# A two-layer decoder trunk on one core: the norm's roots moved behind the projections, x loaded as columns, the sums in two passes, the latents later

## The chip, the core and the metric

The kernel runs on one core of a Trainium2 chip. The core has TensorE (PE in the profile; its weight loads are listed as PEld), VectorE (DVE), ScalarE (ACT), GpSimd (POOL) and SyncE (SP), whose queue issues most of the loads. The engines run their own programs and wait for each other through semaphores. The metric is the device time of one execution in microseconds (us); lower is better.

## The reference

x is (1, 256, 1024) in fp32 and goes through two layers:

```python
h = rms_norm(x, attn_norm[i])
proj = h @ w_in[i]
# A: stick-breaking attention, B: latent attention (MLA), C: sliding window with sinks,
# D: block-sparse (MoBA); 4 heads of 64 each, all from slices of proj
...
x = x + groups.reshape(B, S, MIX_WIDTH) @ w_o[i]
h = rms_norm(x, ffn_norm[i])
u = causal_depthwise_conv(h @ w_up[i], conv_w[i], conv_b[i])
x = x + (jax.nn.silu(u[..., :D_FF]) * u[..., D_FF:]) @ w_down[i]
x = x + (p[i] @ ple_proj[i]) * jax.nn.sigmoid(x @ ple_gate[i])
```

`rms_norm(x, g)` is x times the reciprocal root of its row's mean square, times g. Group A takes z = q k^T / 8, and its weights are exp(log_sigmoid(z) + tail), where tail is the sum of log_sigmoid(-z) over the later keys before the query. Group B projects to a q latent (192) and a kv latent (128), normalises both and projects them up.

## The kernel before

The 256 tokens are two tiles t of 128 rows. The weights come in units of up to 128 x 2048 in fp32, loaded by SP into a ring of six buffers (`raw`), in the order of use. Most products are done in two parts of reduced-width fp32 (fp32r): ACT copies a unit to `wh` (`high(u)`, L539), the high part, and DVE (L1441) or, from the MLP on, POOL (L418) subtracts it from the unit to give `wl` (`low(u)`), which lies where `raw` was. A product is then three matmuls, high by high and the two mixed ones (`split_product`, L859 to L861). Only the units M_MLA_A, M_MLA_B and the one of ple_proj are multiplied whole in fp32, which PE does in two records per matmul. The activations are held as columns: `hT`, with high and low parts `hT_h` and `hT_l`.

There is no scheduler: each engine's order is the order of its program. The places that matter here, in each layer:

- **Start.** SP loads x, the gain row and the weights. ACT squares x (L520), POOL makes the root of each row (L425 to L428), DVE multiplies x by root and gain to `hn` (L1393), PE transposes `hn` (L908), ACT and DVE copy it to `hT`, and PE multiplies the MLA columns (L874) before the first split unit, M_SB_Q. In layer 1 the same chain begins at the end of layer 0, where DVE adds the last term to x (L1733).
- **After M_SB_Q.** PE transposes the convolution's taps (L998) and p (L1005), which were loaded as rows, and the two latents (L1012); then M_SB_K, the MLA up-projection (L1027 to L1029), M_SB_V, M_MOBA_Q, the stick-breaking scores (L1045 to L1054), M_MOBA_K and so on.
- **MLA.** From the up-projection ACT copies q and k/v and squares them, DVE sums the squares (L1599, L1602), POOL takes the power (L410), DVE scales the keys (L1615 to L1620). On DVE `low(6)` and `low(7)`, for M_MOBA_K and M_SWA_Q, stand behind that.
- **Stick-breaking.** ACT makes log(1 + exp(-|z|)) through three tables, DVE adds max(z, 0) (L1629), and PE subtracts the running sums by multiplying with a triangle of -1 (`neg_tri`, L1083, L1089) and with `neg_ones` (L1085), in fp32.

The projections' results leave PSUM through ACT copies (`copied`, L559). Unit numbers: 2 M_SB_Q, 3 M_SB_K, 4 M_SB_V, 5 M_MOBA_Q, 6 M_MOBA_K, 7 M_SWA_Q, 8 M_SWA_KV.

Of the kernel before, what the change touches and what calls it, by code (L numbers as in the profile page):

```python
# [15 lines left out]
P = 128  # L16
# [5 lines left out]
H = 4  # L22
# [22 lines left out]
G_ATTN, G_FFN, G_GROUP = 0, D, 2 * D  # L45
# [56 lines left out]
def _cols(n):  # L102
# [25 lines left out]
    "x_squared": 8, "roots": 12, "hn_ready": 8, "xT_ready": 12, "hT_act": 2, "hT_dve": 2,  # L128
    "xT_high": 12, "xT_low": 12, "pr_ready": 7, "squared": 7, "sums_ready": 4, "ssk_ready": 1,
    "lat_done": 2, "lat_T": 2, "cT_ready": 2, "mla_up": 2, "mla_up_ready": 4, "v_ready": 6,  # L130
    "mla_qk": 2, "mla_T": 2, "mT_ready": 4, "conv_T": 1, "conv_ready": 1, "moba_qk": 1,
# [4 lines left out]
    "sb_log": 3, "sb_soft": 3, "sb_minus": 3, "sb_probs": 3, "groups_T": 4, "mix_ready": 4, "mix_low": 4,  # L136
    "wo_done": 3, "x_mid": 4, "tap2": 4 * STEPS, "tap1": 4 * STEPS, "conv_done": 4 * STEPS,
    "silu": STEPS, "prod": STEPS, "g_high": STEPS, "g_low": STEPS, "p_T": 1, "pT_ready": 1,
    "proj_done": 3, "pp_ready": 4, "down_done": 3, "x_mlp": 4, "gate_ready": 3, "sigmoid": 4, "ple_term": 4,
    "x_done": 4, "tables": 1, "sg_landed": 16, "uq_landed": 16, "uq2_landed": 16,  # L140
    "ukv_landed": 16, "conv_landed": 16, "p_landed": 16, "ng_landed": 16, "gain_landed": 16,
# [28 lines left out]
def build(nc, x_in, p_in, positions, w_in, w_uq, w_ukv, norm_gains, small_gains, w_o, w_up,  # L170
          conv_rows, w_down, ple_proj, ple_gate, out):
    with ExitStack() as ctx:
# [20 lines left out]
        ng = sb("ng", [P, 3 * D])  # L193
# [3 lines left out]
        p_sb = sb("p_sb", [P, TT, PLE])  # L197
# [6 lines left out]
        neg_ones = sb("neg_ones", [P, P])  # L204
        inv_freq = sb("inv_freq", [P, HD // 2])
# [20 lines left out]
        pb = sb("pb", [P, 1536])  # L226
        pt = sb("pt", [P, 1536])
        st = sb("st", [P, ST_ALL])
        conv_raw = sb("conv_raw", [2 * FT, 4, P])
# [12 lines left out]
        sb_e, sb_sp = pb, pt  # L242

# [16 lines left out]
        pos_landed = sem("pos_landed")  # L260
        out_landed = sem("out_landed")
        consts_made = sem("consts_made")
        rope_step, rope_arg, rope_sin = sem("rope_step"), sem("rope_arg"), sem("rope_sin")
# [8 lines left out]
        def load_small(eng, layer):  # L272

            eng.dma_start(sg[:], small_gains[layer].partition_broadcast(P)
                          ).then_inc(F["sg_landed"], 16)
            eng.dma_start(uq[:, 0, :], w_uq[layer][0:P, :]).then_inc(F["uq_landed"], 16)
# [3 lines left out]
            eng.dma_start(conv_raw[:], conv_rows[layer]).then_inc(F["conv_landed"], 16)  # L280
# [36 lines left out]
        def _(sp):  # L317
            for t in range(TT):
                sp.dma_start(x[:, t, :], x_in[0, t * P:(t + 1) * P, :]).then_inc(x_landed[t], 16)
            sp.dma_start(ng[:, 0:D], norm_gains[0, 0:D].partition_broadcast(P)  # L320
                         ).then_inc(F["gain_landed"], 16)
            for layer in range(DEPTH):
# [31 lines left out]
                if layer + 1 < DEPTH:  # L354
                    load_small(sp, layer + 1)
# [19 lines left out]
        def _(pool):  # L375
# [36 lines left out]
            for layer in range(DEPTH):  # L412
# [39 lines left out]
                for t in range(TT):  # L452
                    x_root(0, t)
                if layer == 0:
                    pool.wait_ge(F["roots"], 2)
# [4 lines left out]
                    pool.wait_ge(consts_made, 16)  # L460

# [37 lines left out]
                pool.wait_ge(F["hn_ready"], base["hn_ready"] + 8)  # L499
# [13 lines left out]
        def _(act):  # L513
            act.dma_start(pos_i[:], positions.rearrange("a (t p) -> p (a t)", p=P),
                          allow_slow_non_contiguous=True).then_inc(pos_landed, 16)

# [5 lines left out]

            for i in range(4):
                act.wait_ge(x_landed[i // 2], 16)
# [1244 lines left out]
```

## Time and profile before

| | |
|---|---|
| median of 3 runs | 708.56 us (708.23 to 708.64) |
| the profiled execution's own time | 710.84 us |
| its span, first to last instruction | 709.1 us |
| PE busy | 691.7 us, 98% |
| ACT, POOL, DVE busy | 390.4, 388.7, 331.2 us |
| bytes moved | 116 MB, 164 GB/s |

PE's busy time counts each matmul from its start to its modelled end, and these overlap, so a busy PE doesn't mean that it issues at its peak. The timeline shows when each piece starts. "x12" is the number of records; an fp32 matmul has two. The bracket at the end of a row is the idle time of the engine before it and who ended it.

### The profile page before, as it was taken

The page shows a single profiled execution, that of the slowest core. Times are in us where ns is not written, and L with a number is a line of the kernel's source. Part 1 is how long each engine was busy: PE and PEld are TensorE (multiplying, and loading weights), DVE is VectorE, ACT ScalarE, POOL GpSimd, SP SyncE. Part 2 cuts the span into 40 slices and gives each one's busy share as a digit, 9 for nine tenths or more (in the row PEclk, how much of TensorE's full clock was granted, in tenths as well). Part 3 has the DMA queues.
Part 4 walks back from the last instruction along what each step waited for, and adds up shares of the span by engine and source line. Part 5 has one row for each costly group of instructions (what it writes and reads, how often), then busy time and mean ns, then how long its engine had stood idle before and what let it go on. Part 6 is the DMA issues. An engine that isn't in the chain of part 4 may idle for free.

```text
span 709.1 us, 11731 instructions
## 1 busy us (share of the span) xinstructions
PE 691.7 (98%) x4628; PEld 622.6 (88%) x4628; DVE 331.2 (47%) x548; ACT 390.4 (55%) x578; POOL 388.7 (55%) x213
## 2 busy tenths in 40 slices
PE   4999999999999999999999999999999999999997
PEld 3889998789999999998858999886999999999985
DVE  3746676545433333335165576666343333333333
ACT  4658675466544445555346596546655445545542
POOL 4431200157888888888720222011698888887781
PEclk9999999999999999999999999999999999999999
DMA  9962212465565555554366511326455555555511
GB/s 292 350 226 90 90 60 83 157 229 189 187 196 194 189 178 177 178 184 145 108 208 213 190 60 62 118 82 215 144 183 194 193 179 177 178 183 195 184 31 59
DMA packets 78884, 116.11 MB, mean 164 GB/s; under 512 B 2343, under 2 KB 66727, under 8 KB 78591
## 3 DMA queue, kind: packets, MB, share of 16 engines
q1 hardware_dynamic: 77598, 112.46, 48.0%
q10 hardware_dynamic: 1248, 3.15, 1.1%
q8 instruction: 25, 0.41, 0.2%
q14 instruction: 13, 0.10, 0.0%
HBM read 114.55 MB, written 1.05 MB: 163 GB/s over the span
## 4 chain that ended last, share of the span: by engine, by line
PE 90%; DVE 3%; POOL 3%; ACT 2%; DMA 1%; issue 1%; SPq 0%; DVEq 0%; ACTq 0%
PE ps L859 23%; PE ps L861 23%; PE ps L860 23%; PE ps L874 3%; PE ps L1210 2%; POOL wl L418 2%; PE ps L943 2%; PE ps L980 2%; PE ps L908 1%; PE ps L963 1%; DMA ng<-norm_gains 1%; PE ps L934 1%; PE ps L973 1%; DVE pb L1708 1%; ACT wh L539 1%; DVE wl L1441 1%
## 5 line engine op out<-in xcount | busy, mean ns | idle before, releaser
L418 POOL TENSOR_TENSOR wl<-raw,wh 128x2048 fp32r<-128x2048 f32 (+1 forms) x72 | 324.5, 4539 | 88.0 <-ACT wh L539 88.0
L539 ACT ACTIVATE wh<-raw 128x2048 fp32r<-128x2048 f32 (+1 forms) x102 | 187.6, 1846 | 113.9 <-PE ps L861 107.9
L859 PE MATMUL ps<-hT_h,wh 128*128 128x256 f32 x752 | 213.2, 284 | 0.1
L860 PE MATMUL ps<-hT_l,wh 128*128 128x256 f32 x752 | 212.8, 283 | 0.0
L861 PE MATMUL ps<-hT_h,wl 128*128 128x256 f32 x752 | 212.8, 283 | 0.0
L859 PEld LDWEIGHTS ps<-hT_h,wh 128*128 128x128 f32 x752 | 144.3, 192 | 2.0 <-issue 0.9
L860 PEld LDWEIGHTS ps<-hT_l,wh 128*128 128x128 f32 x752 | 144.3, 192 | 0.6
L861 PEld LDWEIGHTS ps<-hT_h,wl 128*128 128x128 f32 x752 | 144.3, 192 | 0.0
L405 POOL TENSOR_SCALAR st<-st 128x2 f32<-128x2 f32 (+3 forms) x26 | 9.0, 345 | 160.0 <-ACT lat L586 74.6
L859 PE MATMUL ps<-wh,hT_h 128*128 128x256 f32 (+1 forms) x284 | 93.1, 328 | 0.0
L1708 DVE SCALAR_TENSOR_TENSOR pb<-ps,conv,pb 128x255 f32<-128x255 f32 (+1 forms) x96 | 39.7, 475 | 109.6 <-ACT pb L794 109.3
L861 PE MATMUL ps<-wh,hT_l 128*128 128x256 f32 (+1 forms) x284 | 90.2, 318 | 0.0
L860 PE MATMUL ps<-wl,hT_h 128*128 128x256 f32 (+1 forms) x284 | 90.1, 317 | 0.0
L1708 DVE SCALAR_TENSOR_TENSOR pt<-ps,conv,pt 128x255 f32<-128x255 f32 (+1 forms) x80 | 33.1, 476 | 97.3 <-ACT pt L794 97.2
L859 PE MATMUL ps<-wh,gT_h 128*128 128x512 f32 x192 | 75.3, 392 | 0.0
L860 PE MATMUL ps<-wl,gT_h 128*128 128x512 f32 x192 | 74.9, 390 | 0.0
L861 PE MATMUL ps<-wh,gT_l 128*128 128x512 f32 x192 | 74.8, 389 | 0.0
L1441 DVE TENSOR_TENSOR wl<-raw,wh 128x2048 fp32r<-128x2048 f32 (+1 forms) x30 | 64.1, 2148 | 16.3 <-ACT wh L539 16.2
L860 PEld LDWEIGHTS ps<-wl,hT_h 128*128 128x128 f32 x284 | 54.1, 191 | 4.4 <-issue 1.0
L859 PEld LDWEIGHTS ps<-wh,hT_h 128*128 128x128 f32 x284 | 54.1, 190 | 4.4 <-issue 1.0
L861 PEld LDWEIGHTS ps<-wh,hT_l 128*128 128x128 f32 x284 | 54.0, 190 | 3.7
L861 PEld LDWEIGHTS ps<-wh,gT_l 128*128 128x128 f32 x192 | 36.0, 188 | 7.7
(235 smaller groups left out, 895.7 us busy)
## 6 DMA issues: line engine op xcount, KB each, us to landing
raw<-w_up SPq DMA_DIRECT2D x44, 1024.0 KB, 5.1
raw<-w_down SPq DMA_DIRECT2D x22, 1024.0 KB, 4.9
raw<-w_in SPq DMA_DIRECT2D x16, 1024.0 KB, 9.0
raw<-w_o SPq DMA_DIRECT2D x6, 1024.0 KB, 4.9
raw<-ple_gate SPq DMA_DIRECT2D x6, 1024.0 KB, 4.8
raw<-w_in SPq DMA_DIRECT2D x4, 704.0 KB, 6.2
ng<-norm_gains ACTq DMA_DIRECT2D x2, 1024.0 KB, 6.5
raw<-w_o SPq DMA_DIRECT2D x4, 512.0 KB, 3.5
```

Source lines behind the costliest of these rows:

```text
L405: return pool.tensor_scalar(stat(a, n), stat(a, n), 1.0 / width, EPS, ALU.mult, ALU.add)
L418: pool.tensor_tensor(wl[:, slot, 0:n], raw[:, slot, 0:n], wh[:, u % RING, 0:n].bitcast(F32), ALU.subtract).then_inc(ffn_l_made, 1)
L539: act.activation(wh[:, u % RING, 0:n], raw[:, slot, 0:n], ACT.Copy).then_inc(h_made, 1)
L859: pe.matmul(dst, a_h, b_h, start=start, stop=False, skip_group_check=True)
L860: pe.matmul(dst, a_h, b_l, start=False, stop=False, skip_group_check=True)
L861: return pe.matmul(dst, a_l, b_h, start=False, stop=stop, skip_group_check=True)
L874: mm = pe.matmul(o, hT[:, k, tok], raw[:, slot, c], start=k == 0, stop=k == KT - 1, skip_group_check=True)
L943: pe.matmul(o, q(h)[:, P:SEQ], k(h)[:, 0:SEQ], start=(i == 0), stop=False, skip_group_check=True)
L980: mm = pe.matmul(ps[:, bank, 256 + h * HD:256 + (h + 1) * HD], pt[:, c:c + P], v(h, k), start=(k == 0), stop=(k == TT - 1), skip_group_che ...
L1210: mm = pe.matmul(ps[:, PROJ_BANKS[n], :], pT[:, k, t * P:(t + 1) * P], raw[:, slot, c], start=k == 0, stop=k == 1)
L1441: tt(wl[:, slot, 0:n], raw[:, slot, 0:n], wh[:, u % RING, 0:n].bitcast(F32), ALU.subtract).then_inc(l_made, 1)
L1708: stt(o, ps[:, bank + half, j * 256:j * 256 + SEQ - d], conv[:, tap, f], o, ALU.mult, ALU.add).then_inc(F[name], 1)
```

## The change

- **Roots in the copies.** The attention norm is no longer applied to x. `hT` is x as columns times the gain, and the root of a row's mean square is applied to the projections' results: where these have tokens in rows, ACT scales them as it copies (`rooted`, with a scale per row); where they are transposed (M_SB_Q, M_SB_K), DVE multiplies them by a row of roots, which PE makes from a diagonal of -root and `neg_ones`.
- **x as columns.** In layer 0 x is loaded a second time, transposed on the host, straight into `hT`, and DVE multiplies it by the gain there; PE transposes nothing. In layer 1 PE transposes x itself as its quarters are added, and DVE multiplies the gain in as it copies.
- **Embedding and convolution rows as columns.** Both are loaded in their transposed form; PE's transposes of them are gone.
- **Two passes.** The softplus is split into a high part (ACT, `sp_h`) and a low part (DVE, `pt_r`), and each fp32 matmul of the sums becomes two of fp32r.
- **Order of loads.** First half of x as columns, M_MLA_A, second half, M_MLA_B, M_SB_Q, then x by rows, and the small tables each before its use.
- **Latents later.** The latents' transposes stand behind M_SB_K, and the MLA up-projection behind M_SB_V.

```diff
 # SP
-            for t in range(TT):
-                sp.dma_start(x[:, t, :], x_in[0, t * P:(t + 1) * P, :]).then_inc(x_landed[t], 16)
-            sp.dma_start(ng[:, 0:D], norm_gains[0, 0:D].partition_broadcast(P)
-                         ).then_inc(F["gain_landed"], 16)
...
+                    if layer == 0 and u in (M_MLA_A, M_MLA_B):
+                        sp.dma_start(hT[:, k:k + n, :], x_cols[:, k:k + n, :]
+                                     ).then_inc(xT_landed[u], 16)
                     load(rows(w_in, k, n)[:, :, c:c + w], u)
-                    if layer == 0 and u == M_MLA_B:
-                        load_small(sp, 0)
+                    if layer == 0 and u == M_SB_Q:
+                        for t in range(TT):
+                            sp.dma_start(x[:, t, :], x_in[0, t * P:(t + 1) * P, :]
+                                         ).then_inc(x_landed[t], 16)
...
 # ACT
+                def rooted(dst, src, t, name, n, done):
...
+                    act.activation(dst, src, ACT.Identity, scale=stat(ST_X + 6 + t)
+                                   ).then_inc(F[done], 1)
...
                 for t in range(TT):
-                    copied(v_sb[:, t, :], ps[:, t, 0:256], "unit", M_SB_V, "v_ready")
+                    rooted(v_sb[:, t, :], ps[:, t, 0:256], t, "unit", M_SB_V, "v_ready")
                 high(6)
                 high(7)
...
+                for b in range(3):
+                    act.wait_ge(F["sb_soft"], base["sb_soft"] + b + 1)
+                    act.activation(sp_h[b], sb_sp[:, b * 512:(b + 1) * 512], ACT.Copy
+                                   ).then_inc(F["sp_high"], 1)
+                mT_out(0)
                 high(8)
-                mT_out(0)
...
 # PE
-                x_T(hn, AT_START, ("hn_ready", 0), quarters=(0, 1))
...
+                if layer == 0:
+                    pe.sem_inc(F["xT_ready"], 4)
+                    project_tile(M_MLA_A, 0, (0, 1), 0, after=1, part=(0, 1))
...
+                else:
+                    x_T(x, AT_START, None, quarters=(0, 1))
+                    project_tile(M_MLA_A, 0, (0, 1), 0, after=1)
...
                 project_T(M_SB_Q, 2)
 
-                for a in range(4):
-                    mm = pe.transpose(ps[:, 7, a * 44:a * 44 + 44], conv_raw[:, a, :],
...
+                pe.wait_ge(F["diag_made"], base["diag_made"] + 1)
+                pe.matmul(ps[:, 7, 256:512], neg_ones[:], tmp[:, 768:1024], start=True,
+                          stop=True, skip_group_check=True).then_inc(F["row_root"], 1)
+                project_T(M_SB_K, 3)
...
-                project_T(M_SB_K, 3)
+                pe.wait_ge(F["pr_ready"], base["pr_ready"] + 2)
+                project(M_SB_V, (0, 1), 0)
...
-                pe.wait_ge(F["pr_ready"], base["pr_ready"] + 2)
-                project(M_SB_V, (0, 1), 0)
                 pe.wait_ge(F["sbT_ready"], base["sbT_ready"] + 3)
                 project(M_MOBA_Q, (2, 3), 0)
...
-                pe.wait_ge(F["sb_soft"], base["sb_soft"] + 3)
+                pe.wait_ge(F["sp_low"], base["sp_low"] + 3)
...
-                        pe.matmul(o, neg_tri[:], sb_sp[:, i * 256:(i + 1) * 256], start=False,
-                                  stop=False, skip_group_check=True)
...
+                        pe.matmul(o, neg_tri_r[:], sp_h[b][:, j * 256:(j + 1) * 256],
+                                  start=False, stop=False, skip_group_check=True)
+                        pe.matmul(o, neg_tri_r[:], pt_r[:, i * 256:(i + 1) * 256],
+                                  start=False, stop=False, skip_group_check=True)
...
 # DVE
+                dve.wait_ge(F["roots"], base["roots"] + 2)
+                for t in range(TT):
+                    last = ts(tmp[:, 768 + t * P:768 + (t + 1) * P], ident[:],
+                              stat(ST_X + 6 + t), -1.0, ALU.mult, ALU.mult)
+                last.then_inc(F["diag_made"], 1)
+                low(3)
...
+                for b in range(3):
+                    c = slice(b * 512, (b + 1) * 512)
+                    dve.wait_ge(F["sp_high"], base["sp_high"] + b + 1)
+                    tt(pt_r[:, c], sb_sp[:, c], sp_h[b].bitcast(F32), ALU.subtract
+                       ).then_inc(F["sp_low"], 1)
                 low(8)
```

How this stands on the engines. First PE in layer 0 from the end of M_SB_Q to M_MOBA_Q; "..." stands for the matmuls of a product. Before:

```order
L861 MATMUL ps<-hT_h,wl 128x256
L998 MATMUL ps<-ident,conv_raw 128x44 x4
L1005 MATMUL ps<-ident,p_sb 128x128 [waits p_landed]
...
L859 MATMUL ps<-hT_h,wh 128x256 [waits l_made]
...
L1027 MATMUL ps<-uq,lat 128x384 [waits cT_ready,ukv_landed,conv_ready,uq2_landed,pT_ready,uq_landed,consts_made]
L1028 MATMUL ps<-uq,lat 128x384
L1029 MATMUL ps<-ukv,lat 128x512
...
L859 MATMUL ps<-wh,hT_h 128x256 [waits l_made,pr_ready]
...
L859 MATMUL ps<-wh,hT_h 128x256 [waits l_made,sbT_ready]
```

and now (`tmp` holds the diagonal of roots; the product that waits for pr_ready is M_SB_V, the one that waits for sbT_ready M_MOBA_Q):

```order
L1027 MATMUL ps<-tmp,neg_ones 128x256 [waits diag_made]
L877 MATMUL ps<-hT_h,wh 128x256 [waits l_made]
...
L1034 MATMUL ps<-ident,pr 128x128 [waits lat_done]
...
L877 MATMUL ps<-wh,hT_h 128x256 [waits l_made,pr_ready]
...
L1049 MATMUL ps<-uq,lat 128x384 [waits ukv_landed,cT_ready,uq2_landed,rrow_ready,uq_landed,consts_made]
L1050 MATMUL ps<-uq,lat 128x384
L1051 MATMUL ps<-ukv,lat 128x512
...
L877 MATMUL ps<-wh,hT_h 128x256 [waits l_made,sbT_ready]
```

M_SB_V moved from behind the up-projection to ahead of it, so that one product less stands between the up-projection and M_MOBA_K, and the first ten transposes went.

On DVE the steps of the MLA keys and the two `low` behind them (units 6 and 7) stand as they did; before:

```order
L1602 TENSOR_REDUCE st<-tmp 128x8
L1607 TENSOR_TENSOR lat<-lat,sg 128x768 [waits sums_ready]
...
L1615 TENSOR_TENSOR hT<-pr,st 128x8x64 [waits roots]
L1618 TENSOR_TENSOR hT<-hT,sg 128x8x64 [waits dve_step]
L1620 TENSOR_TENSOR hT<-kpe,st 128x8x32
L1441 TENSOR_TENSOR wl<-raw,wh 128x2048 [waits h_made] x2
```

and now:

```order
L1666 TENSOR_REDUCE st<-tmp 128x8
L1671 TENSOR_TENSOR lat<-lat,sg 128x768 [waits sums_ready]
...
L1679 TENSOR_TENSOR hT<-pr,st 128x8x64 [waits roots]
L1682 TENSOR_TENSOR hT<-hT,sg 128x8x64 [waits dve_step]
L1684 TENSOR_TENSOR hT<-kpe,st 128x8x32
L1484 TENSOR_TENSOR wl<-raw,wh 128x2048 [waits h_made] x2
```

Nothing moved within this piece; what it hangs on, the up-projection, is what moved on PE.

## Rows read from the trace of the kernel before

**Rows 1.** The page's busy times and its chain that ended last, by engine.

```profile
PE 691.7 (98%) x4628; PEld 622.6 (88%) x4628; DVE 331.2 (47%) x548; ACT 390.4 (55%) x578; POOL 388.7 (55%) x213
...
PE 90%; DVE 3%; POOL 3%; ACT 2%; DMA 1%; issue 1%; SPq 0%; DVEq 0%; ACTq 0%
```

**Rows 2.** Timeline of PE, 0 to 24.2 us: start, us, what, [idle before].

```profile
9.55 1.94 PE L908 MATMUL ps<-ident,hn 128*128 128x128 f32 x8 [9.55 <-DVE hn L1393]
11.42 5.89 PE L874 MATMUL ps<-raw,hT 128*128 128x352 f32 x12
17.15 1.04 PE L908 MATMUL ps<-ident,hn 128*128 128x128 f32 x8
18.02 6.08 PE L874 MATMUL ps<-raw,hT 128*128 128x352 f32 x20
24.04 0.36 PE L859 MATMUL ps<-hT_h,wh 128*128 128x256 f32 x1
```

**Rows 3.** Timeline of PE's weight loads; one of seven that start 0.59 us apart.

```profile
13.90 0.34 PEld L874 LDWEIGHTS ps<-raw,hT 128*128 128x128 f32 x1 [0.25 <-issue]
```

**Rows 4.** The gain row's transfer in the chain; transfers to 20 us; unit 2's landing.

```profile
1.73 6.90 DMA ng<-norm_gains
...
DMA packets 4205, 5.97 MB, mean 299 GB/s; under 512 B 444, under 2 KB 3520, under 8 KB 4204
...
DMA to landing us min/median/max: 12.1/12.1/12.1
```

**Rows 5.** Timeline of ACT and DVE: wh and wl of unit 2.

```profile
19.66 1.90 ACT L539 ACTIVATE wh<-raw 128x2048 fp32r<-128x2048 f32 x1
...
21.60 2.29 DVE L1441 TENSOR_TENSOR wl<-raw,wh 128x2048 fp32r<-128x2048 f32 x1 [1.10 <-ACT wh L539]
```

**Rows 6.** Timeline of PE between M_SB_Q and M_SB_K, in layer 0 and layer 1.

```profile
29.95 0.44 PE L998 MATMUL ps<-ident,conv_raw 44*128 44x44 f32 x4
...
32.27 0.36 PE L859 MATMUL ps<-hT_h,wh 128*128 128x256 f32 x1
...
377.99 0.44 PE L998 MATMUL ps<-ident,conv_raw 44*128 44x44 f32 x4
...
379.74 0.36 PE L859 MATMUL ps<-hT_h,wh 128*128 128x256 f32 x1
```

**Rows 7.** Timeline of PE: the last up-projection matmul, and M_MOBA_K's first.

```profile
41.54 1.02 PE L1029 MATMUL ps<-ukv,lat 128*128 128x512 f32 x2
...
57.33 0.36 PE L859 MATMUL ps<-wh,hT_h 128*128 128x256 f32 x1
```

**Rows 8.** Timelines of POOL and DVE: the power, the keys, low(6) and low(7).

```profile
48.24 3.02 POOL L410 TENSOR_TENSOR st<-st,neg_half 128x16 f32<-128x16 f32 x1
...
51.59 0.69 DVE L1615 TENSOR_TENSOR hT<-pr,st 128x512 f32<-128x512 f32 x1 [2.63 <-POOL st L439]
...
53.26 4.49 DVE L1441 TENSOR_TENSOR wl<-raw,wh 128x2048 fp32r<-128x2048 f32 x2
```

**Rows 9.** Timeline of PE in the sums; from the chain, ten 64-column records.

```profile
70.67 0.60 PE L1083 MATMUL ps<-pt,neg_tri 128*128 128x256 f32 x2
...
73.29 1.02 PE L1089 MATMUL ps<-pt,neg_tri 128*128 128x512 f32 x2
...
80.07 1.06 PE ps L1100 x10
```

**Rows 10.** Between the layers: DVE, PE, and a stretch (third number from the end: PEclk).

```profile
355.86 0.70 DVE L1733 TENSOR_TENSOR x<-x,hn 128x512 f32<-128x512 f32 x1
...
358.44 1.32 PE L908 MATMUL ps<-ident,hn 128*128 128x128 f32 x8 [1.35 <-DVE hn L1393]
359.87 5.48 PE L874 MATMUL ps<-raw,hT 128*128 128x352 f32 x12
...
372.08 0.35 PE L859 MATMUL ps<-hT_h,wh 128*128 128x256 f32 x1
...
360.30:363.80 3.50, 3.50 (x8) 2.03 (x7) 1.53 (x4) 1.79 (x5) 0.94 (x3) 0.52 1.12 354
```

More of the change, by code:

```diff
@@ L226, in build @@
         pb = sb("pb", [P, 1536])
+        with nc.sbuf_tensor("pt_r", [P, 1536], F32R) as pt_r:
+            pass
         pt = sb("pt", [P, 1536])
         st = sb("st", [P, ST_ALL])
-        conv_raw = sb("conv_raw", [2 * FT, 4, P])
         neg_half = sb("neg_half", [P, 16])
@@ L626, in _ @@
                                    ).then_inc(F["squared"], 1)
-                high(3)
-                if layer == 0:
-                    act.wait_ge(consts_made, 16)
-                for rows, heads in EVEN_ODD:
-                    copied(qk_sb[rows, heads, :],
-                           ps[rows, 2, :].rearrange("p (k n) -> p k n", k=2),
-                           "unit", M_SB_Q, "sbT_ready", scale=HD ** -0.5)
-                copied(pT[:], ps[:, 6, :].rearrange("p (k n) -> p k n", k=2), "p_T", 1, "pT_ready")
                 high(4)
@@ L690, in _ @@
                 for t in range(TT):
-                    copied(pr[:, 1, t, :], ps[:, 2 + t, :], "unit", M_MOBA_K, "pr_ready")
+                    rooted(pr[:, 1, t, :], ps[:, 2 + t, :], t, "unit", M_MOBA_K, "pr_ready")
                 act.wait_ge(F["pr_ready"], base["pr_ready"] + 4)
@@ L904, in x_T @@
                             pe.wait_ge(F[free], base[free] + 2 * t + 2)
-                        pe.wait_ge(F[ready[0]], base[ready[0]] + ready[1] + k + 1)
+                        if ready:
+                            pe.wait_ge(F[ready[0]], base[ready[0]] + ready[1] + k + 1)
+                        else:
+                            pe.wait_ge(F["x_done"], 4 * (layer - 1) + k + 1)
                         for j in range(4):
@@ L1589, in _, with sb_rooted @@
                     last.then_inc(F["lat_done"], 1)
-                dve.wait_ge(F["conv_T"], base["conv_T"] + 1)
-                dve.tensor_copy(conv[:], ps[:, 7, 0:176].rearrange("p (a n) -> p a n", a=4)
-                                ).then_inc(F["conv_ready"], 1)
-                low(4)
+                dve.wait_ge(F["row_root"], base["row_root"] + 1)
+                dve.tensor_copy(rrow[:], ps[:, 7, 256:512]).then_inc(F["rrow_ready"], 1)
+                def sb_rooted(rows, heads, bank, scale):
+                    c = ps[rows, bank, :].rearrange("p (k n) -> p k n", k=2)
+                    stt(qk_sb[rows, heads, :], c, scale,
+                        rrow[rows].unsqueeze(1).broadcast_to([rows.stop - rows.start, 2, SEQ]),
+                        ALU.mult, ALU.mult).then_inc(F["sbT_ready"], 1)
+                if layer == 0:
+                    dve.wait_ge(consts_made, 16)
+                dve.wait_ge(F["rrow_ready"], base["rrow_ready"] + 1)
+                unit_done(dve, layer, M_SB_Q)
+                for rows, heads in EVEN_ODD:
+                    sb_rooted(rows, heads, 2, HD ** -0.5)
+                unit_done(dve, layer, M_SB_K)
+                sb_rooted(slice(0, P), slice(H, H + 2), 3, 1.0)
                 low(5)
```

255 lines of the change are left out of this document (145 added, 110 removed).

## Prediction

> **What bounds the kernel now.** I read the page first: PE is busy 98% of a span of 709.1 us and carries 90% of the chain that ended last [rows 1]. PE's busy time is no measure of slack by itself, since pipelined matmuls overlap, so I went on to PE's timeline and asked of every stretch that the diff touches: when does PE start it, what does it issue there, and which engine's result comes last. Outside these stretches (output projection, MLP, gate) neither the work nor its order changes, so their time is taken as it is.
>
> PE's losses are few. The first transposes start at 9.55 us, the first product (the MLA columns) at 11.42, the first split product (unit M_SB_Q) at 24.04 [rows 2]. Between the layers PE waits 1.35 us for hn [rows 10]. The rest is work, so an edit pays only where it lets PE start earlier or issue less, and it costs where PE comes to a product whose wl part is not there.
>
> **Start of layer 0.** Before, x (1 MB) and the gain row (0.5 MB) land before the first weights. Now the first half of x as columns (0.5 MB) and the first weight unit (0.7 MB) are the first in the queue. The gain row, with 1.6 MB up to and with it, landed at 8.6 us [rows 4], so 1.25 MB should be there at about 7.5 us, and PE can start its first product then instead of at 11.42. Loads are issued in order and the queue holds the rest back: the third unit, issued at 7.06 us, took 12.1 us to land, at 19.2, with 5.1 MB issued up to and with it, against 5.97 MB moved in the first 20 us [rows 4]. In the new order 3.5 MB stand up to and with it, 1.6 MB less at 0.3 MB per us: it lands at about 14.4. ACT then makes wh in 1.90 us and DVE wl in 2.29 [rows 5]: ready at 18.7.
>
> PE's own path: 32 records of the MLA product. While PE had just started, a record took 0.59 us (the weight loads stand 0.59 us apart), later 0.30 (20 records in 5.98 us) [rows 2, 3]. The granted clock is printed as full there, but the spacing is that of the half level, 1.2 GHz, until about 15.7 us. From 7.5 us with a slow stretch of some 5 us and full speed behind it, PE needs 5 + (32 - 8.5) x 0.30 = 12 us, so it is at M_SB_Q at about 19.5, behind the 18.7 of DVE. **Start: 24.04 to 19.5, -4.5 us** (bounds: -3.0 if the slow records go on to 15.7 us as before and the third unit lands 1.5 us later; -5.3 if DVE's 18.7 is the end). The squares of x, the roots and the diagonal come behind the third unit's wh on ACT, about 5 us after it, and PE needs the diagonal only a product (5.8 us, 24.04 to 29.9 [rows 2, 6]) later: hidden, with about a microsecond to spare.
>
> **Between M_SB_Q and the next products.** In layer 0, 2.4 us pass from the end of M_SB_Q (29.9) to M_SB_K (32.27), with eight transposes of conv and p, six of the latents and waits for them [rows 6]. Six transposes stay (eight take 17.15 to 18.02 [rows 2], so 0.11 us each, 0.65). The new fp32 matmul of 256 columns for the row of roots has the shape of those of L1083, 0.44 us a piece; four of them with their 128-column partners take 2.62 [rows 9]. So 2.4 - 0.65 - 0.45 = **-1.3 us in layer 0**, and in layer 1, where the same stretch is 1.85 us (377.9 to 379.74), **-0.75 us**.
>
> **The MLA up-projection one product later.** This speaks against the change. From the last up-projection matmul (41.54) a chain runs over all engines: ACT copies and squares, DVE sums, POOL takes the power (48.24, 3.02 us), DVE scales the keys (51.59) and only then subtracts for units 6 and 7, since low(6) stands behind the keys on DVE: 4.49 us for two, so unit 6 is there at 53.26 + 2.29 = 55.5 [rows 7, 8]. That is 14.0 us after 41.54. PE comes to unit 6 (M_MOBA_K) at 57.33, 15.8 us after 41.54, with M_SB_V, M_MOBA_Q and the stick-breaking scores between: 1.8 us of slack. The new order puts M_SB_V ahead of the up-projection, so PE has only 15.8 - 5.8 = 10.0 us of work in that gap, while nothing in the chain gets shorter: ACT's squares don't wait for v_sb in either version, and v_sb and the wh of unit 6, which do get earlier, aren't last. PE should stand still for **4.0 us at M_MOBA_K, in each layer**. What is queued behind it on PE, the key product, its transposes and everything else, moves with it. Bounds: 0 if a step of the chain isn't needed where I read it, 4.5 if what is new on ACT and DVE ahead of the chain's first step delays it.
>
> What does such a wait do to PE's clock? Ahead of 359.87 us PE had 1.35 us idle, transposes and a short wait. From 360.3 to 363.8 the granted clock is 0.52, the lower of its two levels, 1.2 GHz, and twelve records took 5.5 us instead of 12 x 0.30 = 3.6 [rows 10]: 1.9 us lost, of which 0.1 to 0.2 is the modelled tail, so 1.8. A wait of 4 us is longer than that one, so I expect a half-speed stretch after each. Part of it may fall into the wait itself, so I take 1.2 us each, between 0 and 1.8: **+2.4 us in two**. The Trainium skill (TensorE: Matmul & The Clock Gate, Part 1) says that idleness takes the array to half clock and activity releases it; by its rule the lower bound of 0 falls away, and the trace agrees at the one place where it can be seen.
>
> **Stick-breaking sums.** Before, from 70.67 to the end of L1089's matmul at 74.15: four pairs in 2.62 us and one of 512 columns, 0.86 [rows 9]. Now each fp32 matmul becomes two of fp32r. The split products are of that type: 48 of 256 columns in 5.8 us, 0.12 each [rows 2, 6], so 0.24 at 512. At 128 columns no row of that type exists. The shortest fp32 matmuls in the trace, with 64 columns, follow each other at 0.11 us a record (ten in 1.06 us [rows 9]), as the 128-column ones do (0.22 for the two records of one), so the weight load seems to set it: I take 0.11. Bounds 0.06 (half the 256-column time) and 0.22 (no gain over fp32). Sum 4 x (0.24 + 0.22) + 0.48 = 2.3 us: **-1.2 us a layer**, between -0.3 and -1.6.
>
> The added copies on ACT (three, 0.6 us each) and subtractions on DVE (three, 0.7) stand ahead of wh and wl of unit 8, and PE waits for both. They cost nothing because the wait at M_MOBA_K comes first: in it ACT and DVE get ahead with the softplus. By my sum the last low part and wl of unit 8 are then ready some 0.3 us before PE comes to each. If that wait isn't there, this cover is gone too, and about 0.5 us a layer comes back.
>
> **Between the layers.** Before: the gate ends at 356.9 (358.44 less the idle time and the pipeline's tail), transposes of hn at 358.44 after the root, first product at 359.87, M_SB_Q at 372.08 [rows 10]. Now x is transposed as soon as it is added. The third addition on DVE ends at 356.56 [rows 10], so transposes run from 356.95, DVE scales the first quarter until 358.2 and PE starts the product there. 32 records at 0.30 and the eight transposes that are left, 0.9, are 10.5 us: M_SB_Q at about 368.7, if the clock holds, with wl of unit 2 ready some 0.3 us earlier. **-3.4 us** with the clock held, -1.6 without; PE idles only 0.4 us there, so I take the first.
>
> **Sum.** -4.5 - 1.3 + 4.0 - 1.2 = -3.0 in layer 0, -3.4 - 0.75 + 4.0 - 1.2 = -1.35 in layer 1, and 2.4 for the clock: -1.95 us. Against the profiled execution, whose span is 709.1 and whose own time is 710.84, that is a span of 707.15. The median of the three runs is 708.56, 2.3 under the profiled execution's time; taken from it, the forecast is **706.6 us**. About 0.2%, or 1.4 us (707.1 to 710.0), is what a measurement can tell from no change.
>
> **The rivals.**
> - *The waits come, the clock holds* (or drops once, cheaply): -1.95 - 2.4 = -4.35, so 704.2. For it: matmuls are dense ahead of the wait. Against: rows 10.
> - *No wait at M_MOBA_K*: the chain isn't bound to the up-projection as I read it. -4.35 - 8.0 = -12.35, with 1 us given back at the sums: 697.2. Against it: 14.0 against 10.0 us is a wide gap.
> - *The early gain is smaller*: the third unit lands 1.5 us later, or the clock still drops between the layers (+1.8): about 708.3, no change. The Trainium skill (TensorE: Matmul & The Clock Gate, Part 4) says that transposes don't count as activity for the gate; the trace shows a drop after a stretch mostly of them, and with its rule the drop would stay, and the time be that of this rival.
> - *Slower*: the two waits cost more than themselves. If PE comes out of each wait at half clock and needs two such stretches to get back, each costs 3.6 instead of 1.2, together +4.8: 711.4. It decides from 2.9 us a wait, where the sum passes +1.4. For it: the start shows some 4 us of slow records in a row. Against: between the layers one stretch was enough.
>
> **How the numbers follow.** Forecast 706.6 (705.2 to 708.2) 42%; clock holds 22%; smaller early gain 20%; no wait 8%; slower 8%. Range 701.5 to 709.6: it leaves out the slower rival and the case without a wait, and takes in all bounds of the start and the sums. Faster by over 0.2%: 0.61 (0.28 of the forecast's 0.42, the 0.22, the 0.08, 0.03 of the third); within: 0.31; slower: 0.08.
>
> **What would show it.** PE's first product at about 7.5 us and M_SB_Q at 19.5; an idle time of PE of about 4 us before M_MOBA_K in both layers, released by DVE's wl; a granted clock near 0.5 behind each and none between the layers; the sums in 2.3 us; M_SB_Q of layer 1 some 11.8 us after the gate's end instead of 15.2. If PE shows no wait at M_MOBA_K, the largest term is wrong; if M_SB_Q starts after 21 us, the loads are.

## The result, and the profile after

| | before | changed |
|---|---|---|
| median, us | 708.56 | 710.84 |
| profiled execution: span, us | 709.1 | 711.1 |
| profiled execution: mean granted clock | 0.997 | 0.990 |

The ratio is 1.0035, with a 95% interval of 1.0027 to 1.0044: the change costs 0.35%. The forecast was 706.6 us, with a range up to 709.6. The time lies outside it, on the side of the rival that had 8%. Of 17 executions of the changed kernel one took 1744 us, at a mean clock of 1.00; no trace of it exists, and it stands in none of the counts below.

The page's busy times and clock digits of the changed kernel stand beside [rows 1]:

```profile
PE 687.7 (97%) x4600; PEld 622.2 (87%) x4600; DVE 336.6 (47%) x560; ACT 390.1 (55%) x576; POOL 390.0 (55%) x213
...
PEclk9998999999999999999999899999999999999999
```

PE is busy for 4 us less and the span is 2 us longer. In the clock row (40 slices of 17.8 us, tenths of full speed) the digit 8 stands at two places, 53 to 71 and 391 to 409 us (the second stretch runs on into the next slice, see below). The waits of PE (what waited, for whom, us in total, times, longest) say where the rest went:

```profile
PE ps L891 <- DVE hT L1586: 9.5, 1, 9.5
PE ps L877 <- DVE wl L1484: 7.7, 2, 3.8
PE ps L1274 <- ACT hT_h L568: 0.9, 2, 0.5
PE ps L891 <- DVE hT L1419: 0.4, 1, 0.4
```

The second line is new: two waits of 3.85 us at M_MOBA_K, as the forecast had them. The first is the start: PE's first product begins at 9.49 us and not at 7.5. Now the timelines, which answer to [rows 2, 4, 5]. Of the start (DVE, ACT, then PE):

```profile
8.66 1.29 DVE L1586 TENSOR_TENSOR hT<-hT,gcol 128x512 f32<-128x512 f32 x2 [8.66 <-DMA gcol<-attn_cols]
...
16.65 1.89 ACT L552 ACTIVATE wh<-raw 128x2048 fp32r<-128x2048 f32 x1
...
18.58 2.29 DVE L1484 TENSOR_TENSOR wl<-raw,wh 128x2048 fp32r<-128x2048 f32 x1 [2.20 <-ACT wh L552]
...
9.49 12.39 PE L891 MATMUL ps<-raw,hT 128*128 128x352 f32 x32 [9.49 <-DVE hT L1586]
21.46 0.55 PE L877 MATMUL ps<-hT_h,wh 128*128 128x256 f32 x1
```

gcol, the gain as columns (8 KB), landed at 8.66 us. The first weights, issued at 1.26 and 7.3 us on their way, landed at about 8.6, also after the forecast's 7.5; DVE's multiplication by gcol then held PE until 9.49. From there PE took the 12.0 us of the forecast to M_SB_Q. The bytes moved in 40 slices of half a microsecond, 0 to 20 us:

```profile
GB/s 0 0 0 66 205 205 221 205 131 17 15 195 367 380 424 423 410 398 381 394 400 386 381 391 373 354 371 395 395 393 426 377 375 363 352 348 346 361 370 377
```

From 4.5 to 5.5 us almost nothing moves, though weights and the second half of x's columns still wait to be loaded.

PE around M_MOBA_K of layer 0, and the clock there (columns of the last two lines: stretch, its length, PE's busy time and matmuls, granted clock, DMA share, GB/s), against [rows 7, 10]:

```profile
43.50 1.02 PE L1051 MATMUL ps<-ukv,lat 128*128 128x512 f32 x2
...
57.56 0.58 PE L877 MATMUL ps<-wh,hT_h 128*128 128x256 f32 x1 [3.85 <-DVE wl L1484]
...
65.67 0.60 PE L1083 MATMUL ps<-ident,lat 128*96 128x128 f32 x4
...
55.90:62.70 6.80, 5.14 (x24) 0.50 0.00 0
...
404.04:410.80 6.76, 4.87 (x23) 0.50 0.00 1
```

From the last up-projection matmul to M_MOBA_K 14.06 us pass (forecast: 14.0). The clock is at its lower level, 1.2 GHz, for 6.8 us at each wait, twice as long as between the layers before. The first stretch begins at 55.9 us, 1.7 us before PE starts M_MOBA_K, so 5.1 us of it fall on work. M_MOBA_K takes 8.1 us instead of 5.8.

DVE in the same stretch shows the chain of [rows 8], unchanged, 2.0 us later: the keys after POOL's power, and low(6) behind them.

```profile
53.55 0.69 DVE L1679 TENSOR_TENSOR hT<-pr,st 128x512 f32<-128x512 f32 x1 [2.63 <-POOL st L456]
...
55.22 4.49 DVE L1484 TENSOR_TENSOR wl<-raw,wh 128x2048 fp32r<-128x2048 f32 x2
```

The sums, against [rows 9]: from 73.08 to the next product at 75.48, 2.4 us (forecast 2.3), no wait in them.

```profile
73.08 0.36 PE L1104 MATMUL ps<-gT_h,neg_tri_r 128*128 128x256 f32 x1
73.28 0.29 PE L1106 MATMUL ps<-pt_r,neg_tri_r 128*128 128x256 f32 x1
73.40 0.22 PE L1108 MATMUL ps<-gT_l,neg_ones_r 128*128 128x128 f32 x1
73.46 0.28 PE L1110 MATMUL ps<-pt_r,neg_ones_r 128*128 128x128 f32 x1
73.58 0.33 PE L1104 MATMUL ps<-gT_h,neg_tri_r 128*128 128x256 f32 x1
```

Between the layers, against [rows 10]:

```profile
358.20 1.03 PE L928 MATMUL ps<-ident,x 128*128 128x128 f32 x8
359.68 2.60 PE L891 MATMUL ps<-raw,hT 128*128 128x352 f32 x8 [0.44 <-DVE hT L1419]
...
370.01 0.37 PE L877 MATMUL ps<-hT_h,wh 128*128 128x256 f32 x1
...
361.00:364.00 3.00, 3.00 (x16) 1.00 1.10 358
```

M_SB_Q starts 11.8 us after the gate's end, as forecast, and the clock holds.

**Where the difference arises.** Start times of PE, changed less before, in the two profiled executions: M_SB_Q -2.6 (forecast -4.5); M_MOBA_K of layer 0 +0.2, behind the sums +1.3, M_SB_Q of layer 1 -2.1, M_MOBA_K of layer 1 +1.1, end +2.0.

**The clock of single executions.** The mean granted clock differs from execution to execution, and a stretch of 3.5 us at half level is 0.0025 of it (3.5 / 2 / 709). Of 19 executions of the kernel before, 14 have 0.999 or 1.000 and spans of 706.3 to 707.1, one 0.998 (707.5), four 0.997 (708.5 to 708.8). So the drop between the layers of [rows 10] is in few of them, and the profiled execution was one. Changed kernel: seven have 0.995 (two stretches, spans around 708.2), three 0.993 (708.8), six 0.990 (four stretches, around 710.8). The profiled execution is of the last kind. This turns out to be a part of the miss. Only the profiled executions show where their clock is low; the counts of stretches of the others are worked out from the mean, which also takes in the end of the span: in the kernel with matmuls in the wait, below, the profiled execution has 0.998, and only its last 2.3 us are low, when PE has nothing left to do.

### The profile page after: what moved, and what is told of

It reads as the page before. It is cut to its first block, busy times and chain, and to the rows that moved or that the text cites. A ratio compares the mean times of both kernels' runs of the same rounds, so it can differ in the third digit from the quotient of the medians.

```text
span 711.1 us, 11689 instructions
## 1 busy us (share of the span) xinstructions
PE 687.7 (97%) x4600; PEld 622.2 (87%) x4600; DVE 336.6 (47%) x560; ACT 390.1 (55%) x576; POOL 390.0 (55%) x213
## 4 chain that ended last, share of the span: by engine, by line
PE 92%; DVE 2%; POOL 2%; ACT 1%; DMA 1%; issue 1%; ACTq 0%; DVEq 0%
PE ps L877 24%; PE ps L878 24%; PE ps L879 24%; PE ps L891 3%; PE ps L1237 2%; PE ps L963 2%; PE ps L1000 2%; PE ps L983 1%; DMA gcol<-attn_cols 1%; PE ps L954 1%; POOL st L427 1%; PE ps L993 1%; PE ps L928 1%; POOL wl L435 1%; DVE wl L1484 1%
## 5 line engine op out<-in xcount | busy, mean ns | idle before, releaser
L877 PE MATMUL ps<-wh,hT_h 128*128 128x256 f32 (+1 forms) x284 | 94.7, 333 | 7.7 <-DVE wl L1484 7.7
L878 PE MATMUL ps<-wl,hT_h 128*128 128x256 f32 (+1 forms) x284 | 92.1, 324 | 0.0
L879 PE MATMUL ps<-wh,hT_l 128*128 128x256 f32 (+1 forms) x284 | 92.0, 324 | 0.0
L877 PEld LDWEIGHTS ps<-wh,hT_h 128*128 128x128 f32 x284 | 56.2, 198 | 12.1 <-DVE wl L1484 8.2
L878 PEld LDWEIGHTS ps<-wl,hT_h 128*128 128x128 f32 x284 | 56.3, 198 | 4.0 <-issue 0.5
L879 PEld LDWEIGHTS ps<-wh,hT_l 128*128 128x128 f32 x284 | 56.1, 198 | 3.6
L879 PEld LDWEIGHTS ps<-wh,gT_l 128*128 128x128 f32 x192 | 36.1, 188 | 7.7
```

The costliest lines, as they stand in the source:

```text
L877: pe.matmul(dst, a_h, b_h, start=start, stop=False, skip_group_check=True)
L878: pe.matmul(dst, a_h, b_l, start=False, stop=False, skip_group_check=True)
L879: return pe.matmul(dst, a_l, b_h, start=False, stop=stop, skip_group_check=True)
```

## The experiments

The theory after the two traces: the miss has three parts, gcol at the start, the clock behind the waits, and the drop between the layers that the profile of before had and its median had not. The rivals: the added steps on ACT and DVE cost more than seen, or the wait at M_MOBA_K isn't due to the order on PE. Every ratio is to the kernel before, which took 708.4 to 708.5 us beside these runs.

### One product moved, in the kernel before

```diff
+                pe.wait_ge(F["pr_ready"], base["pr_ready"] + 2)
+                project(M_SB_V, (0, 1), 0)
                 if layer == 0:
                     pe.wait_ge(consts_made, 16)
...
-                pe.wait_ge(F["pr_ready"], base["pr_ready"] + 2)
-                project(M_SB_V, (0, 1), 0)
                 pe.wait_ge(F["sbT_ready"], base["sbT_ready"] + 3)
```

> The kernel before with one part of the change alone: M_SB_V ahead of the MLA up-projection on PE. Theory 1: a wait of about 4 us at M_MOBA_K in each layer and a half-speed stretch behind each, 2 x (4.0 + 2.4): 708.6 + 12.8 = 721.4, or somewhat less, since PE's wait gives ACT and DVE cover later. Rival (the wait in the changed kernel comes from its new work on ACT and DVE and not from the order): under 712.

Measured: 720.61 us, ratio 1.0174 (1.0150 to 1.0198). PE's timeline at M_MOBA_K, the clock behind it in both layers, and PE between the layers with the clock there:

```profile
60.26 0.39 PE L859 MATMUL ps<-wh,hT_h 128*128 128x256 f32 x1 [3.84 <-DVE wl L1441]
...
61.10:64.60 3.50, 3.50 (x20) 0.52 0.00 0
412.60:416.10 3.50, 3.50 (x20) 0.53 0.00 0
...
362.85 1.32 PE L908 MATMUL ps<-ident,hn 128*128 128x128 f32 x8 [1.35 <-DVE hn L1393]
...
375.54 0.36 PE L859 MATMUL ps<-hT_h,wh 128*128 128x256 f32 x1 [0.44 <-DVE wl L1441]
...
364.30:367.70 3.40, 3.40 (x12) 1.00 1.10 351
```

This part alone costs 12.1 us: two waits of 3.84, and two stretches or four at half clock. The same wait is followed by one stretch here and by two in the changed kernel's profile; the four executions have 0.995, 0.994 (span 717.7) and twice 0.990 (720.2). The number of stretches is not a property of the kernel. Nor is the drop between the layers: this trace has the transposes and the 1.35 us idle of [rows 10], and the clock holds. M_SB_Q then follows the transposes after 12.69 us instead of 13.64, and would be earlier still if it didn't wait 0.44 us for wl. The wait at M_MOBA_K belongs to the order on PE, not to what the change put on ACT and DVE.

### Matmuls in the wait

In the changed kernel PE fills the wait with products into a part of PSUM that nobody reads; nothing else changes.

```diff
                 mm.then_inc(F["sb_z"], 1)
+                for i in range(28):
+                    pe.matmul(ps[:, 2, 256:512], hT_h[:, i % 8, 0:P], hT_h[:, (i + 1) % 8, :],
+                              start=True, stop=True, skip_group_check=True)
                 project(M_MOBA_K, (2, 3), 256)
```

> The changed kernel with 28 extra matmuls of 256 columns (3.4 us of work whose result is overwritten) on PE between the stick-breaking scores and M_MOBA_K, where it otherwise waits 3.9 us. The wait itself stays, only PE isn't idle in it. Theory 1 (idleness drops the clock, and each drop costs 2.4 us): the granted clock stays full through M_MOBA_K and the time falls by 2 x 2.4 = 4.8, to 706.0. Rival (the slow stretch isn't tied to idleness, or costs nothing since other engines are the bound there): no change, 710.8.

Measured: 707.08 us, ratio 0.9977 (0.9968 to 0.9987). M_MOBA_K, the sums behind it, and the clock behind it in both layers:

```profile
56.56 0.39 PE L877 MATMUL ps<-wh,hT_h 128*128 128x256 f32 x1 [0.46 <-DVE wl L1487]
...
69.84 0.36 PE L1107 MATMUL ps<-gT_h,neg_tri_r 128*128 128x256 f32 x1
...
56.60:60.00 3.40, 3.40 (x28) 1.00 0.00 0
402.80:406.20 3.40, 3.40 (x29) 1.00 0.00 0
```

The wait for wl is 0.46 us in each layer, M_MOBA_K starts 36.1 us after M_SB_Q as it did, and no stretch at half clock is left while PE works. So the clock alone costs 710.84 - 707.08 = 3.8 us in the median, not 2.4. Ten executions have spans of 705.1 to 706.3. Against these, the changed kernel's executions with two stretches (708.2) lose 2.9 us, and those with four (710.8) 5.5. The traces say how much of this is the clock: from M_MOBA_K to the sums PE takes 13.3 us here (56.56 to 69.84) and 15.5 in the changed kernel (57.56 to 73.08), in layer 1 13.3 and 15.4. That is 2.2 us for each double stretch, 4.4 in two. The other 1.0 us between the two profiled executions stands ahead of M_SB_Q, which starts at 20.45 here and at 21.46 there. Why the start differs so between executions, and whether it does in the unprofiled ones with four stretches, is not shown.

### Half as many

> The changed kernel with 14 instead of 28 extra matmuls ahead of M_MOBA_K; the extra matmuls write a part of PSUM that nobody reads. They take 14 x 0.12 = 1.7 us of the wait of 3.85 us, so PE idles for 2.2 us and comes to M_MOBA_K at the same time as before. Theory A (2.2 us without work is enough for the clock to fall, as 1.35 us and transposes were between the layers): half speed behind each wait, 709.5 to 711 us. Theory B (the clock falls only behind the longer wait): it holds, 707.1 us as with 28.

Measured: 709.70 us, ratio 1.0008 (0.9997 to 1.0019).

```profile
51.92 1.91 PE L1078 MATMUL ps<-hT_h 128*128 128x256 f32 x14
55.96 0.39 PE L877 MATMUL ps<-wh,hT_h 128*128 128x256 f32 x1 [2.13 <-DVE wl L1487]
...
56.10:59.70 3.60, 3.60 (x19) 0.53 0.00 0
404.50:407.90 3.40, 3.40 (x18) 0.50 0.00 0
```

Theory A holds: the clock falls behind 2.13 us without work too, with one stretch in each layer here; the ten executions have 0.995 (four, two stretches) and 0.997 (six, one). From M_MOBA_K to the sums the single stretch costs 1.5 us in each layer (14.8 us against 13.3). With 3.85 us idle there were two to four stretches in two layers, with 0.46 none. A longer wait costs more than its length, but in steps and not each time.

### Unit 6 split ahead of the keys

In the changed kernel DVE makes the low part of unit 6 while it waits for POOL's power, instead of behind the keys. It idles 2.63 us there.

```diff
                     ).then_inc(F["mla_qk"], 1)
+                low(6)
                 dve.wait_ge(F["roots"], base["roots"] + 4)
...
-                low(6)
                 low(7)
```

> The changed kernel with one line moved: on DVE low(6), the wl of M_MOBA_K, stands ahead of the wait for POOL's power instead of behind the keys. Theory 1 (the wait of 3.9 us at M_MOBA_K in each layer, and the half-speed stretch behind it, are what ate the gain): both waits and both clock drops go, 2 x (3.9 + 2.4) = 12.6 us, of which about 1 us a layer comes back because ACT and DVE lose their cover at the sums and the stick-breaking weights: 710.8 - 12.6 + 2 = about 700. Rival (PE has another operand that comes as late, such as the keys or wl of unit 7, so the wait only moves): 708 or more.

Measured: 700.26 us, ratio 0.9878 (0.9861 to 0.9894). DVE, then PE, then PE's waits:

```profile
50.07 2.29 DVE L1484 TENSOR_TENSOR wl<-raw,wh 128x2048 fp32r<-128x2048 f32 x1
52.78 0.69 DVE L1680 TENSOR_TENSOR hT<-pr,st 128x512 f32<-128x512 f32 x1 [0.43 <-POOL st L456]
...
52.75 0.36 PE L877 MATMUL ps<-wh,hT_h 128*128 128x256 f32 x1
...
PE ps L1104 <- DVE pt_r L1704: 0.3, 2, 0.2
```

wl is there at 52.36, 0.4 us before PE comes; the keys are as early as they were. One line on another engine takes away both waits (7.7) and the clock's loss (3.8); the median falls by 10.6 us, 0.9 less than the two together. At the sums a wait of 0.18 us in layer 0 and 0.17 in layer 1 appears, the cover that the forecast said would go with the wait (it had put 0.5 on it). The other 0.6 us is not traced; the start alone differs by more than that from execution to execution.

### M_SB_V behind the up-projection again

The other way to take the wait away: the order on PE of before, in the changed kernel.

```diff
-                pe.wait_ge(F["pr_ready"], base["pr_ready"] + 2)
-                project(M_SB_V, (0, 1), 0)
                 if layer == 0:
                     pe.wait_ge(consts_made, 16)
...
+                pe.wait_ge(F["pr_ready"], base["pr_ready"] + 2)
+                project(M_SB_V, (0, 1), 0)
                 pe.wait_ge(F["sbT_ready"], base["sbT_ready"] + 3)
```

> The changed kernel with M_SB_V behind the MLA up-projection again, as before; low(6) stays behind the keys. Theory: PE has 5.8 us more work between the up-projection and M_MOBA_K, the wait of 3.85 us a layer is gone with the stretch at half clock behind it, and PE comes to M_MOBA_K some 1.5 us after wl is ready: about 700.3 us, as with unit 6 split early. Rival (the wait comes from what the change put on ACT and DVE, not from the order on PE): a wait stays, over 704 us.

Measured: 702.20 us, ratio 0.9908 (0.9891 to 0.9924). The waits at M_MOBA_K are gone, as the theory said, but it is 1.9 us behind the kernel with unit 6 split early, where the same time was expected. PE shows why: a new wait at the up-projection.

```profile
32.40 0.81 PE L1034 MATMUL ps<-ident,pr 128*128 128x128 f32 x6
34.05 0.88 PE L1047 MATMUL ps<-uq,lat 128*128 128x384 f32 x2 [0.83 <-ACT lat L577]
...
PE ps L1047 <- ACT lat L577: 1.7, 2, 0.8
```

Without M_SB_K or M_SB_V between the transposes of the latents and the up-projection, PE waits 0.83 us for ACT's copies, twice. This is what the moved product is good for in the new order: it covers these copies. In the kernel before, M_SB_K stood between the transposes and the up-projection, so there the move had nothing to cover. The forecast had seen only its cost.

### The gain columns first

```diff
+            act.dma_start(gcol[:], attn_cols).then_inc(gcol_landed, 16)
             act.dma_start(pos_i[:], positions.rearrange("a (t p) -> p (a t)", p=P),
                           allow_slow_non_contiguous=True).then_inc(pos_landed, 16)
-            act.dma_start(gcol[:], attn_cols).then_inc(gcol_landed, 16)
```

> The changed kernel with the gain column (8 KB) issued ahead of the positions (256 elements of 4 bytes) on ACT's queue. Its landing at 8.66 us is what DVE's first multiplication waited for. Theory A (it stands behind the positions' small pieces): it lands at about 6 us, and PE starts when the first weights are there, at 8.6 to 9: up to 0.9 us gained, 710. Theory B (the whole transfer system is slow there whatever the order, as nearly nothing is moved from 4.3 to 5.3 us in the trace): no change.

Measured: 710.83 us, ratio 1.0019 (1.0006 to 1.0032), no change in the median. DVE, PE, and the bytes moved from 0 to 20 us:

```profile
5.92 1.29 DVE L1586 TENSOR_TENSOR hT<-hT,gcol 128x512 f32<-128x512 f32 x2 [5.92 <-DMA gcol<-attn_cols]
...
7.76 12.23 PE L891 MATMUL ps<-raw,hT 128*128 128x352 f32 x32 [7.76 <-DMA raw<-w_in]
19.56 0.55 PE L877 MATMUL ps<-hT_h,wh 128*128 128x256 f32 x1
...
GB/s 0 0 0 57 148 290 200 181 206 216 215 285 260 332 447 434 366 383 406 398 379 391 385 379 352 365 399 410 393 393 418 354 369 348 348 346 356 385 385 357
```

gcol lands at 5.9 instead of 8.66 us, the hole at 4.5 us is gone, and now the first weights are what PE waits for: they land at 7.76, 0.8 us earlier too. M_SB_Q starts at 19.56: the forecast's 7.5 and 19.5 us, but for one DMA's place in a queue. The other traces bear this out and give its size. In the five with the positions first, gcol lands at 7.5 to 8.7 us, PE starts at 8.45 to 9.49 (in three it waits for gcol, in two for the weights) and M_SB_Q at 20.05 to 21.46. In the four with gcol first, gcol lands at 5.9 to 6.2, PE starts at 7.76 to 8.15, always as the weights land, and M_SB_Q at 18.84 to 19.56. The median of this run hides it. Executions with the same clock show it: at 0.995 the median span is 707.55 (four) against 708.2, at 0.990 709.35 (six) against 710.75, so 0.7 to 1.4 us. Six of these ten had 0.990, of the changed kernel's 16 only six, and that difference is enough to eat the gain.

### Both edits

> The changed kernel with both edits: unit 6 split ahead of the keys (700.26 us alone) and the gain columns issued ahead of the positions. Alone, the second edit brought the span of the profiled run from 711.1 to 709.1, but the medians did not move. Theory: the gain columns were what PE's first product waited for, and the median of the run with this edit alone only hid that, because the clock behind the two waits fell for one stretch in some executions and for two in others. Without the waits the clock is steady, and the edit must show: 698.8 to 699.4 us, PE's first product at about 7.8 instead of 8.9 us. Rival (in unprofiled executions the gain columns are not last, nothing to gain): 700.3 us.

Measured: 698.93 us, ratio 0.9859 (0.9840 to 0.9878); spans of 696.8 to 697.7. With no waits for the clock to fall behind, the second edit is worth 1.3 us. The clock is not the same in all four, 1.000 twice and 0.998 twice (spans 696.8 and 697.0, 697.4 and 697.7); the profiled one has 1.000. This kernel is 9.6 us faster than the one before and the best of all here.

### The sums in one pass again

On top of both edits, `neg_tri` and `neg_ones` in fp32 on `sb_sp` as before, without the copies and subtractions.

```diff
-                        pe.matmul(o, neg_tri_r[:], sp_h[b][:, j * 256:(j + 1) * 256],
-                                  start=False, stop=False, skip_group_check=True)
-                        pe.matmul(o, neg_tri_r[:], pt_r[:, i * 256:(i + 1) * 256],
-                                  start=False, stop=False, skip_group_check=True)
...
+                        pe.matmul(o, neg_tri[:], sb_sp[:, i * 256:(i + 1) * 256], start=False,
+                                  stop=False, skip_group_check=True)
```

> Both edits, and the stick-breaking sums in one fp32 pass again, with ACT's three copies and DVE's three subtractions for them left out. Theory: PE's sums take 1.1 us longer a layer (3.5 instead of 2.4), and the waits of 0.15 us a layer for the last low part go: 2 x 1.1 - 0.3 = +1.9 us on the kernel with both edits, so 700.9 if that is 699.0. Rival (six steps of 4 us in all on ACT and DVE delay wl of unit 8 or a later wait, so that two passes bring nothing once the wait ahead of M_MOBA_K is gone): equal to or below the kernel with both edits.

Measured: 700.51 us, ratio 0.9882 (0.9863 to 0.9902): 1.6 us over the kernel with both edits, 0.8 a layer. The two passes pay, net of the waits for the last low part.

### All of x before the first transpose

```diff
                 else:
+                    pe.wait_ge(F["x_done"], 4 * layer)
                     x_T(x, AT_START, None, quarters=(0, 1))
...
-                    if layer + 1 < DEPTH and b == 2:
+                    if layer + 1 < DEPTH and b == 3:
```

> Both edits, but in layer 1 PE waits for all four quarters of x before the first transpose, and DVE scales the first two behind the last addition. The fourth addition ends some 1.3 us after the third, the transposes of the first half and the scaling follow: PE idles some 2.5 us instead of 0.4. Theory: +2 us if the clock holds, +4 if it falls between the layers as it did before: 701 to 703 us. Rival (the early transposes bring nothing, DVE's split of unit 2 is what M_SB_Q waits for anyway): equal to the kernel with both edits.

Measured: 702.13 us, ratio 0.9901 (0.9882 to 0.9919), 3.2 us over both edits.

```profile
352.16 1.26 PE L928 MATMUL ps<-ident,x 128*128 128x128 f32 x8 [2.14 <-DVE x L1804]
353.69 0.93 PE L891 MATMUL ps<-raw,hT 128*128 128x352 f32 x1 [0.28 <-DVE hT L1420]
...
352.50:356.10 3.60, 3.33 (x11) 0.56 1.10 356
```

PE idles 2.4 us instead of 0.4, and in the profiled execution a stretch at half clock follows; the other three have the same mean of 0.998, which fits one stretch but doesn't prove it. So the early transposes are worth the 2.0 us of idle time that they save, and the 1.2 that is left goes, as far as the one trace shows, to the clock.

## Why the prediction was wrong

**The start, -4.5, was too large:** by 1.9 us in the profiled execution, by about 1.0 in the middle one of the five traces with this order. The step "1.25 MB should be there at about 7.5 us, and PE can start its first product then" counted bytes in SP's queue and left out that DVE first multiplies by gcol, which stands on ACT's queue behind the positions, a transfer of 256 pieces of four bytes. gcol landed at 8.66 us; with gcol ahead of the positions it landed at 5.9, and PE started at 7.76. The count of bytes failed by itself as well: with the positions first the weights were there at 8.45 to 8.6 us and not at 7.5, since almost nothing moved for a microsecond. The rest of this step held: 12 us to M_SB_Q. In executions with equal clock the miss is 0.7 to 1.4 us, in the kernel with both edits 1.3. Two slips did no harm. The forecast's own numbers give 13.9 and not 14.4 us for the landing of unit 2 (19.2 less 1.6 MB at 0.3 MB per us); it landed at about 14.5. And its wh was taken as made from there on, but ACT came to it at 16.65, behind a table load and four small activations, so wl was ready at 20.87 and not at 18.7. That is still 0.6 us before PE, and with gcol first, where PE comes at 19.56, ACT's steps moved too and wl was ready at 19.19.

**Between M_SB_Q and the next products, -1.3 and -0.75: right.** From M_SB_Q to the last up-projection matmul, M_SB_V left out, PE takes 16.24 us (21.46 to 43.50, less 5.8) where it took 17.50 ([rows 2, 7]), -1.3 us; in layer 1 it is -0.9. (It is eight transposes that went here, four of the convolution's taps and four of p, not ten.)

**The wait at M_MOBA_K, 4.0 us in each layer: right,** 3.85 measured, and its cause too: the move alone makes it (3.84), low(6) ahead of the keys takes it away. The forecast named the line that stood in the way, "low(6) stands behind the keys on DVE".

**The clock, +2.4: too small.** "I take 1.2 us each, between 0 and 1.8" came from the one stretch of [rows 10]. For one stretch behind a wait that is near: 1.4 to 1.5 us in the traces. But a wait is followed by one stretch or by two, and two cost 2.2, because part of the first falls into the wait, as the forecast thought it might. Against the kernel with matmuls in the wait the changed one loses 3.8 us in the median. The upper bound of 3.6 for both, and the range with it, didn't take in what the slower rival described as "two such stretches". The rival had the number of stretches right in 6 of 16 executions, judged by their mean clock, and its price of 3.6 us a wait too high. That [rows 10] had one stretch behind a short idle time said nothing on how many follow a long one. The Trainium skill (TensorE: Matmul & The Clock Gate, Part 1) says that idle time takes the array to 1.2 GHz; the traces agree (0.50 behind 3.85 us, and behind 2.13 us), though the drop between the layers before, behind 1.35 us and transposes, came in one trace and not in the other.

**The sums, -1.2 a layer: right,** 2.4 us instead of 3.5, of which 0.8 a layer stays where the waits are gone.

**Between the layers, -3.4: right for the profiled execution, not for the median.** M_SB_Q came 11.8 us after the gate's end instead of 15.2. But the profiled execution of the kernel before has the stretch at half clock of [rows 10], which 14 of 19 executions, by their mean clock, don't have, and these are 1.9 us shorter. The step that failed is the one that looked harmless: "The median of the three runs is 708.56, 2.3 under the profiled execution's time; taken from it". Of the 2.3 us, 1.9 go with that stretch; what the change saved by removing it, the median had never paid. The kernel before with one product moved, whose trace lacks the stretch, shows where such a part lies: 1.0 us between the transposes and M_SB_Q of layer 1, and 0.5 at the start, where M_SB_Q comes at 23.58 instead of 24.04. The clock held, though transposes stand there as before: what the forecast weighed of the Trainium skill (TensorE: Matmul & The Clock Gate, Part 4), that the drop would stay, did not show: eight transposes and 0.44 us idle, and 1.00 granted from 361 to 364 us.

**The sum again, in spans.** A median execution before has 706.7. Less 3.0 and 1.35 for the two layers of the forecast, plus 1.8 that it can't save, plus 1.3 for gcol's place, is 705.45; the kernel with matmuls in the wait, which has all but the clock's loss, shows 705.3. Plus 3.8 for the clock is 709.1 to 709.2, and a median execution of the changed kernel has 709.1. The miss of 4.2 us is thus 1.8 + 1.3 + 1.4 = 4.5, to 0.3. The first and the last of the three are differences between executions, and in the profiled executions a part of each stands at the start and not at a stretch.

What stays open: what decides in one execution whether one or two stretches follow a wait, why the start differs by over a microsecond, and why the changed kernel's and the gain-first kernel's shares of the two differ.

## What to carry to other kernels

Before an edit is priced against a profile, look at the clock of the other executions: a stretch at half clock that the profiled one has and most others don't is no gain to be had. When a step is put later on the engine that bounds the kernel, work out the chain behind it, and look for the one item on another engine that stands behind that chain without needing it: here one line moved on DVE turned a loss of 2.3 us into a gain of 8.3. And of a start, follow each operand to its own queue; 8 KB issued behind a transfer of tiny pieces took 6.1 to 7.4 us to land, and 5.1 to 5.3 when issued first.

## What the runs showed of the hardware

- A wait of 3.85 us on PE cost 3.85 and, in the median, 1.9 more (3.8 in two). In the traces the granted clock stayed at 0.5 for some 3.4 us or for 6.8, and at waits of the same 3.84 to 3.85 us it did the one and the other; PE's work behind them took 1.4 to 1.5 us longer with the one and 2.2 with the other. With 1.35 us idle and eight transposes it fell in one trace and held in another.
- With the positions (256 pieces of four bytes) first on ACT's queue, all queues together moved 17 and 15 GB/s in the two slices from 4.5 to 5.5 us, and an 8 KB transfer issued at 1.30 us landed at 8.66. With the 8 KB first there is no such hole (216 and 215 GB/s), and it landed at 5.92, issued at 0.80. The hole is in all five traces with the one order and in none of the four with the other. That the small pieces make it is not shown: with gcol first they are moved as well, and there is no hole.
- Four fp32r passes, two of 256 and two of 128 columns, take 0.46 us (73.58 to 74.04 us), where the 256-column ones of the products take 0.12 each: the 128-column ones are hardly shorter, 0.11.
